# Turning softmax probabilities with a scaled diagonal in place of the identity

## The reference

```python
logits = jnp.einsum('bqngd,bqknd->bqngk', qg, k_sel).astype(jnp.float32) * dh ** -0.5
logits = jnp.where(valid[:, :, None, None, :], logits, -jnp.inf)
attn = jax.nn.softmax(logits, axis=-1).astype(v.dtype)
o = jnp.einsum('bqngk,bqknd->bqngd', attn, v_sel)
```

## Time and profile before

| | |
|---|---|
| median of 3 runs | 1605.23 us (1603.8 to 1605.49) |
| profiled execution | 1604.69 us, span 1602.9 us |
| granted TensorE clock, mean | 0.989 |
| PE busy | 1544.2 us (96%) |
| DVE busy | 871.3 us (54%) |
| ACT busy | 683.5 us (43%) |
| POOL busy | 265.5 us (17%) |
| DMA | 140.24 MB, mean 87 GB/s |

### The profile page before, as it was taken

The page is one execution under the profiler, slowest core; times in us unless marked ns, Lnnn a source line. Parts: engine busy times, 40 slices in busy tenths (PEclk is TensorE's granted clock), DMA queues, the critical chain, the costliest instruction groups (busy, mean ns, idle before and its releaser), DMA issues.

```text
span 1602.9 us, 30655 instructions
## 1 busy us (share of the span) xinstructions
PE 1544.2 (96%) x11764; PEld 1407.4 (88%) x11772; DVE 871.3 (54%) x1564; ACT 683.5 (43%) x995; POOL 265.5 (17%) x466
## 2 busy tenths in 40 slices
PE   6999989999999999999999998899999999999998
PEld 5787745999999999999978775579999999999997
DVE  6568883345555553223857788624455555522345
ACT  4445455344444442224444445634544444322241
POOL 4120340111111110000123106102111111101000
PEclk8999999999999999999999999999999999999999
DMA  4233044223222223222223312333223323333221
GB/s 144 91 105 94 27 138 111 59 74 92 88 87 86 87 80 110 86 86 80 80 70 110 107 40 75 105 82 93 80 82 89 91 83 89 98 88 91 83 77 61
DMA packets 225719, 140.24 MB, mean 87 GB/s; under 512 B 13122, under 2 KB 219604, under 8 KB 225552
## 3 DMA queue, kind: packets, MB, share of 16 engines
q1 hardware_dynamic: 223220, 133.46, 28.9%
q0 software_dynamic: 2400, 5.42, 1.1%
HBM read 131.21 MB, written 7.65 MB: 87 GB/s over the span
## 4 chain that ended last, share of the span: by engine, by line
PE 81%; DVE 12%; issue 3%; ACT 3%; SPq 0%; DMA 0%; DVEq 0%; POOL 0%; ACTq 0%; POOLq 0%
PE ps L1728 24%; PE ps L1730 23%; PE ps L1729 23%; DVE score L1393 3%; DVE m L1390 3%; DVE w_L L1278 1%; PE ps L2084 1%; DVE aL L1290 1%; PE ps L2013 1%; PE ps L1755 1%; DVE Lb L1465 1%; PE ps L1812 1%; PE ps L1924 1%; PE ps L2168 1%; DVE stat L1512 1%
## 5 line engine op out<-in xcount | busy, mean ns | idle before, releaser
L1278 DVE TENSOR_TENSOR w_L<-w_raw,w_H 128x1024 fp32r<-128x1024 f32 (+4 forms) x236 | 256.8, 1097 | 421.0 <-ACT w_H L897 418.3
L1728 PE MATMUL ps<-bH,w_H 128*128 128x272 f32 x1664 | 481.0, 289 | 4.6 <-DVE w_L L1278 3.2
L1730 PE MATMUL ps<-bH,w_L 128*128 128x272 f32 x1664 | 479.5, 288 | 0.0
L1729 PE MATMUL ps<-bL,w_H 128*128 128x272 f32 x1664 | 477.7, 287 | 0.0
L897 ACT ACTIVATE w_H<-w_raw 128x1024 fp32r<-128x1024 f32 (+4 forms) x236 | 220.2, 943 | 297.7 <-PE ps L1730 287.9
L1728 PEld LDWEIGHTS ps<-bH,w_H 128*128 128x128 f32 x1664 | 312.5, 188 | 6.3 <-DVE w_L L1278 4.1
L1729 PEld LDWEIGHTS ps<-bL,w_H 128*128 128x128 f32 x1664 | 313.5, 188 | 0.1
L1730 PEld LDWEIGHTS ps<-bH,w_L 128*128 128x128 f32 x1664 | 312.6, 188 | 0.0
L1728 PE MATMUL ps<-actH,w_H 128*128 128x272 f32 x704 | 204.2, 290 | 0.0
L1730 PE MATMUL ps<-actH,w_L 128*128 128x272 f32 x704 | 203.7, 289 | 0.0
L1729 PE MATMUL ps<-actL,w_H 128*128 128x272 f32 x704 | 202.7, 288 | 0.0
(11 more groups left out here) (351 smaller groups left out, 2333.2 us busy)
## 6 DMA issues: line engine op xcount, KB each, us to landing
w_raw<-in_w_up SPq DMA_DIRECT2D x88, 512.0 KB, 3.7
w_raw<-in_w_down SPq DMA_DIRECT2D x32, 512.0 KB, 3.8
w_raw<-in_w_in SPq DMA_DIRECT2D x24, 512.0 KB, 5.5
w_raw<-in_w_ple_gate SPq DMA_DIRECT2D x16, 512.0 KB, 3.9
w_raw<-in_w_down SPq DMA_DIRECT2D x16, 384.0 KB, 3.4
w_raw<-in_w_out SPq DMA_DIRECT2D x16, 320.0 KB, 3.5
w_raw<-in_w_in SPq DMA_DIRECT2D x8, 452.0 KB, 4.9
w_raw<-in_w_in SPq DMA_DIRECT2D x8, 384.0 KB, 3.4
```

The lines of the kernel that those rows point to most:

```text
L1278: ins = dve.tensor_tensor(w_L[u % SPLIT][:, a:b], w_raw[raw_slot(l, u)][:, a:b], w_H[u % SPLIT][:, a:b].bitcast(F32), ALU.subtract)
L1728: pe.matmul(out, wh, xh, start=start, stop=False)
L1729: pe.matmul(out, wh, xl, start=False, stop=False)
L1730: return pe.matmul(out, wl, xh, start=False, stop=stop)
```

## The change

The probabilities stay as the exponentials left them. VectorE multiplies the identity by the reciprocal sums instead, into a new tile `diag` (one 128x128 block for each of six turns in flight), and TensorE multiplies the blocks of probabilities by this diagonal with an ordinary product in place of a transpose by the identity. From `u` = 3 VectorE waits for the turn that last read the same block of `diag`. The tile lies over blocks 6 and 7 of `aL`.

```diff
@@ -163,6 +163,10 @@
         r_col = sb("r_col", [P, TILES])
+        turn_scale = ExitStack()
+        sb("scale_skip", [P, (KD + 6) * T], F32, turn_scale)
+        diag = sb("diag", [P, 6, P], F32, turn_scale)
+        turn_scale.close()
         whole = ExitStack()
@@ -1520,8 +1524,10 @@
                     for n in range(2):
-                        pr = prob_of(u, n)[:, 0:P * (t + 1)]
-                        dve.tensor_scalar(pr, pr, stat[:, s, 3, n:n + 1], None, ALU.mult).then_inc(q_norm, 1)
+                        m = 2 * u + n
+                        if u >= 3:
+                            dve.wait_ge(pt_mm, at(pt_mm, m - SOFT + 1))
+                        dve.tensor_scalar(diag[:, m % SOFT, :], ident, stat[:, s, 3, n:n + 1], None, ALU.mult).then_inc(q_norm, 1)
@@ -2000,7 +2006,8 @@
                     for b in range(m // 6 + 1):
-                        mm = pe.transpose(ps[:, TURN_BANK[m % 3], P * b:P * b + P], prob_of(m // 2, m % 2)[:, P * b:P * b + P], ident)
+                        mm = pe.matmul(ps[:, TURN_BANK[m % 3], P * b:P * b + P], prob_of(m // 2, m % 2)[:, P * b:P * b + P],
+                                       diag[:, m % SOFT, :], start=True, stop=True)
                     mm.then_inc(pt_mm, 1)
```

## The result

The changed kernel takes 1612.99 us (median of nine runs, 1608.9 to 1614.62) against 1608.4 for the kernel before in the same comparison (nine runs, 1603.19 to 1611.15): a ratio of 1.0033, 95% interval 1.0017 to 1.0049. It is slower by 0.33%, or 5.3 us; the two medians themselves stand 4.6 us apart. The forecast was +5.8 us, or +0.36%. The first three of the nine runs before are those shown ahead of the prediction, 1603.8 to 1605.49; with the other six the kernel before spreads over 8 us. The predicted 1610.5 stood on the low end of that.

A forecast was written before the change was run, and what follows sets the result against it. TensorE was taken to bound the kernel, VectorE the softmax stretches up to 226 us. Layer 0 2.8 + 0.5 = 3.3, layer 1 2.8 - 0.3 = 2.5: +5.8 on 1604.7 gives 1610.5 us, range 1607.2 to 1613.5.

The forecast's parts named there:

- the price of a block: TensorE's turns: an f32 product takes two passes, 0.22 us a block in place of 0.11, so +0.11 us.
- the blocks that count: TensorE's path in each softmax stretch: 0.66 + 0.16 + 1.54 + 0.44 = 2.8 us a layer; other turns mostly hidden.
- the base under it: Whole kernel before: 1604.7 us, the profiled execution, to which the sum adds +5.8.
- the half clock of layer 0: Pair of turns at 219.84 us, under half clock: about +0.5 comes through, nothing gained from VectorE; layer 0 +3.3.
- the stretch between the layers: Outside the two softmax stretches: the sum includes no change in time there.
- dearer: Rival, TensorE's turns: weight loads of 190 ns set the pace, 0.38 us a block, 1619 us; chance 0.05.
- the gaps take more: Rival, softmax stretches: TensorE's waits hide all but the 14 blocks, 2 x 1.54 = 3.1, 1607.8 us; chance 0.12.
- VectorE's pace decides to the end: Rival, softmax stretches: VectorE's 2.3 us a layer comes through whole, added passes lie in TensorE's waits, 1600.1 us; chance 0.07.
- What VectorE gives back: Narrower multiplies save VectorE 2.3 us a layer, only tile 1's 0.4 where it bounds: -0.3 in layer 1, layer 0 nothing.
- the new waits: VectorE's 18 new waits on pt_mm a layer: dispatch only, 0.1 us taken for the six of tile 1.
- the clock stays up: Rival, softmax stretch: more matmul work keeps TensorE at 2.4 GHz, layer 0's 3.3 becomes 2.5, 1609.7 us; chance 0.08.

The follow-up runs named there:

- e4: Kernel before, with ordinary products with the identity for the turns of tiles 2 and 3 only: 1612.36 us in one run, beside 1605.66.
- e1: Kernel before, with all turns as ordinary products with the identity, VectorE's scaling untouched: 1613.28 us against 1605.66, ratio 1.0045.
- e9: Changed kernel with probabilities and diagonals typed as f32r, so one pass for a product: 1607.33 us against 1605.79, ratio 1.0.
- e2: Changed kernel with the transpose by the identity put back, the diagonal made but not used: 1605.98 us, ratio 0.9998.
- e6: Kernel before, with diagonal and product for tile 1 only and no new wait: 1607.14 us against 1607.73, ratio 0.9997.
- e10: Changed kernel with every turning product issued twice into the same place: 1632.7 us in one run.
- e7: Changed kernel with eight keep-warm products filling TensorE's wait for VectorE at the start of layer 1: 1611.97 us, ratio 1.0032.
- e3: Kernel before, with ordinary products with the identity for the turns of tiles 0 and 1 only: 1604.38 us in one run, beside 1605.66.
- e8: Kernel before, with eight keep-warm products filling TensorE's wait for VectorE at the start of layer 1: 1607.57 us, ratio 1.0003.
- e5: Kernel before, with three keep-warm products in place of two after each of steps 0 to 4: 1609.9 us in one run, beside 1607.73.

## Why the prediction was right on the path and wrong in its time

In short: the price of a block and the blocks that count came out as forecast. Three steps of the sum failed: the base under it (1604.7, measured 1608.4), the half clock of layer 0 (+3.3 for the layer, measured +2.40), and the stretch between the layers, which the sum has at nothing (+2.8 in the profile). In the medians the base is 3.7 too low and the change 1.2 smaller than forecast, which leaves the 2.5 us by which the time is off. In the two profiled executions -0.9 in layer 0 and some +2.8 between the layers turn the forecast 5.8 into 7.6.

**A block costs 0.11 us more.** Right. 28 records in 3.12 us (forecast 3.1 to 3.2), 12 in 1.34 (1.3), 240 records of 275 ns. The pace read off the starts held; the duration of the records would have said nothing. What the Trainium skill ("TensorE: Matmul & The Clock Gate", Terms) states of the transpose mode, 4x faster for FP32, is not what the runs show if it is read as pace: 0.223 against 0.116 us, a factor of 1.9. A second price set by the load of weights (the rival "dearer") didn't appear either.

**Which blocks count.** Right, nearly term by term. Between the same starts on TensorE in layer 0:

| TensorE from ... to ... | before | after | more | forecast |
|---|---|---|---|---|
| logits of step 9, logits of step 10 (6 blocks) | 3.69 | 4.37 | 0.68 | 0.66 |
| logits of step 11 (6 blocks before a wait) | 2.82 | 2.94 | 0.12 | 0.16 |
| turns at the 14 blocks | 1.51 | 1.50 | 0 | 0 |
| 14 blocks, up to the turns of the cache's keys | 1.62 | 3.13 | 1.51 | 1.54 |
| last product with V but one | 0.97 | 0.96 | 0 | 0 |
| last turn (the turns beside ScalarE's copies) | 5.35 | 5.35 | 0 | 0 |
| first index product (4 blocks) | 0.55 | 1.06 | 0.51 | 0.44 |

Sum +2.80, forecast 2.8, in both layers. e4 puts all of it in tiles 2 and 3, e1 gives it without VectorE's side, e9 takes it away by taking one pass away. This rules out the rival "the gaps take more". "VectorE's pace decides to the end" falls with e2, where VectorE's savings leave the second halves at 16.51.

**What VectorE gives back.** Right in size: -0.3 forecast, -0.29 to -0.40 measured; e6 alone shows -0.41 and -0.45, e2 -0.18 and -0.47. These are single executions, and whole halves scatter: 22.29 to 23.00 us with wide multiplies and 21.90 to 22.66 with narrow ones, medians 22.85 and 22.48 (without the two halves in which the half clock cost something, and without e10). The copy that starts 0.24 us earlier in all twelve narrow stretches is the firm part of it. The term of 0.1 us for the new waits has no counterpart: the copy starts at 16.99 us in e6, which has none of them, and at 17.02 in the changed kernel.

**The half clock in layer 0: a step that failed.** The sum takes the half clock of the profile before as given in the changed kernel, with +0.5 for it and nothing from VectorE: 3.3. The profile has no half clock in either stretch, so layer 0 got VectorE's gain and gave +2.40. The size of the term is right where the clock does fall: e7, the changed kernel outside its fill, has the half clock in layer 0, with +0.59, and e3 +0.56. What was wrong is that the fall would stay. It goes with the change more than the chance of 0.08 for the rival "the clock stays up" allows: of the eight first halves with f32 products in all turns (after, e1, e7, e10) one has a half clock, of the ten with transposes or one-pass products in tiles 0 and 1 (before, e2, e4, e8, e9) all have, of the six in between (e3, e5, e6) three. That is the rival's own reason, more matmul work there, with this many traces behind it and no experiment on the cause of a fall. The two stretches together gave +4.9 in the profile; with the half clock in layer 0 they would give 2.80 + 0.59 + 2.51 = +5.9.

**Between the layers: a term set at nothing.** The prediction lets the kernel's time move only inside the stretches. The profile moved by 2.8 us outside them, by two more falls of the clock.

**The base: the step behind the miss in time.** The change was forecast at +5.8 (+0.36%), the ratio says +0.33% (1.0017 to 1.0049, that is 2.7 to 7.9 us). Direction and size hold. The time itself, 1612.99, is 2.5 above the forecast of 1610.5. The prediction set the sum on 1604.7, "0.5 under the median of the runs", as if three runs within 1.7 us showed the kernel's level. Nine runs of the same kernel have a median of 1608.4 and a spread of 8 us. The forecast +5.8 on that base would be 1614.2, 0.7 above the upper end of the range; that 1612.99 lies in the range is luck, since the two medians happen to be only 4.6 us apart. In other comparisons the kernel before had 1605.66, 1607.73 and 1605.79. The range had bounds for each cost of the change and none for the base, though the profile showed that the clock falls in places of this kernel.

## What to carry to other kernels

Before a transpose on TensorE is turned into a product that does more, count the records that one product of that type leaves, and take the pace from their starts: in f32 it is two passes for one, and what is saved on another engine must be on the chain in the same part of the stretch to pay for it. Cut a stretch at the point where the chain changes its engine; before it only VectorE's part counted here, behind it only TensorE's. Where the clock falls in some executions and not in others, compare stretches cut at starts, add up the time at half clock in each before a difference is put down to a change, and give the base a spread of its own. A fall seen in the profile before is no fixed part of the kernel: the change can move it.

## What the runs showed of the hardware that I had not expected

**A fall of the clock costs half its length where TensorE bounds, and nothing where VectorE does.** Between the stretches, 3.4 us at half clock cost 1.5 to 2.0 us, and three such falls 4.7 to 5.1; up to VectorE's first copy of the stretch they cost nothing. Behind the same wait of 1.87 us the clock stayed at 1.00 in the kernel before and fell twice in the changed one; it fell there once in e5, which has the transposes of the kernel before. This makes a part of the spread of the times: over the 29 runs of the kernel before beside e5 to e8 the granted clock and the time go together with a correlation of -0.57, which is about a third of their variance. What makes the rest isn't shown.

**The first half may hang on when a fill of GpSimd starts.** The first half of layer 1 took 21.90 us in e7, 0.65 less than in the changed kernel, with the same instructions. The timelines of GpSimd and VectorE in e7:

```profile
1008.12 0.36 DVE L1547 COPY a_tmp<-featT 64x32 f32<-64x32 f32 x2
...
1011.28 0.74 POOL L821 MEMSET qbm<- 128x768 f32 x1 [4.00 <-DMA out_pool_p<-u_tok]
```

and in the changed kernel:

```profile
1010.17 0.35 DVE L1547 COPY a_tmp<-featT 64x32 f32<-64x32 f32 x2
...
1011.60 0.74 POOL L821 MEMSET qbm<- 128x768 f32 x1 [2.26 <-DMA out_pool_p<-u_tok]
```

The fill waits for a DMA; it starts 3.16 us behind VectorE's first copy in e7 and 1.43 behind it in the changed kernel. In e1, whose layer 1 has the other short first half (22.29), it is 2.99, and in e8's layer 1 (22.57) 1.87; in the kernel before 1.15 and 1.36. The late fills go with the short halves (not in e10, where it is 2.90 and more and the doubled products set the pace). No kernel here moved the fill alone, so this is read from the traces and not shown by an experiment.
